# Splitting the softplus of a stick-breaking attention for its triangular sums, with GpSimd's sum, the remainder's product and linear attention's pieces placed anew

## The chip, the cores and the metric

The kernel runs on one core of a Trainium2 chip. The metric is the device time in microseconds of that core; the time before is the median of three executions. Five engines matter: TensorE (PE in the profile, its weight loads are PEld), VectorE (DVE), ScalarE (ACT), GpSimd (POOL) and SyncE (SP), which issues most of the DMAs. Each engine works off its own instructions in order, and engines wait for each other on semaphores.

## The reference, cut to what matters

One layer of a hybrid block over 1024 frames of width 1024: a projection feeds three groups of heads (stick-breaking attention, RWKV-7, gated linear attention), then an output projection and a feed-forward part. The change lies in the stick-breaking attention, with gated linear attention woven into the same loops:

```
z = jnp.einsum('bqhd,bkhd->bhqk', q_blk, kh) * scale
mask = key_pos[None, :] < q_pos[:, None]
log_1m_beta = jnp.where(mask, jax.nn.log_sigmoid(-z), 0.0)
between = lax.cumsum(log_1m_beta, axis=3, reverse=True) - log_1m_beta
weights = jnp.where(mask, jnp.exp(jax.nn.log_sigmoid(z) + between), 0.0)
...
o_intra = jnp.einsum('bhts,bhsv->bhtv', scores, v_c)     # linear attention, 64-frame chunks
S = S * jnp.exp(b_last)[:, :, 0, :, None] + jnp.einsum('bhsk,bhsv->bhkv', k_c * jnp.exp(b_last - b), v_c)
```

With softplus(z) = -log_sigmoid(-z), the weight of a key is exp(z minus the sum of softplus over this key and all later ones). The sum inside a block of 128 keys is a product with a triangular matrix of -1, and the sum over later blocks is a product with a matrix of -1 (`ones`) of a running sum `R`.

## The kernel before, in words

The program has three stages in time: the front (projection and RWKV-7), `heads` (both attentions), and `back` (output projection and feed-forward). `back` is another block of the program and starts when all engines have left `heads`.

`heads` treats the six heads as three pairs (`PAIRS`, index `i`). A pair has 24 units (`UNITS`, index `u`): first 8 units for the first 512 queries, then 16 for the second 512. A unit is one block of 128 keys (`kb`, from the last to the first) for one head of the pair. The blocks on the diagonal are masked and narrower, so a unit is 128, 256, 384 or 512 columns wide (`off` is the first column): per pair 2 each of 128, 256 and 384 wide in either half of the queries, the rest 512 wide, which makes 12 of 512 and 4 of each other width. `span(u)` is the unit's columns.

What each engine does for a unit, in its order:

* TensorE: `scores(u+2)` puts z into one of four PSUM banks `Z`, as two products with operands of type fp32r (`qL`, `qH`) and a mask product; `sums(u)` adds the triangular product of `SP` and, unless the unit is the head's first, the `ones` product of `R`, all in plain f32; then for even `u` `values(u-2)`; then its pieces of linear attention, `gla(i * NU + u)`.
* ScalarE: `exp_of_z(u+2)`, `weight(u)` (the exponential of the finished bank), `log_of_e(u+2)`, then other pieces and its `gla`.
* VectorE: `softplus(u)` (from `E` and the bank `Z` into `SP`), from `u` = 10 of the last pair on one `split_low` of the output projection's operands a unit (`ahead`), at u = 7 and 11 of later pairs `scale` and `mixed_low`, and its `gla`.
* GpSimd: the running sum, `R` new = `R` old + `SP`, a cleared block beside it on the diagonal, a drain, the semaphore `cut`, and its `gla`.

A semaphore counts units: `z`, `log`, `sp` (softplus), `tri_mm` (all sums of a unit in PSUM), `sum` and `cut` (GpSimd), `weight`.

Linear attention is cut into labelled pieces, each with a slot number in the table `SLOTS`; it is done twice (`h` = 0, 1, one for each half of the frames), the second 26 slots later (`LAG`). `gla(n)` issues on an engine all its pieces whose slot is at most `n`. So a slot is a unit, counted through the pairs (24 a pair). Pieces that this text names: on VectorE `scan` 5, `diag0`, `diag1` 7, 8, `qin`, `kout` 8, `keys3` 14, `take0`, `take1` 14, 15, `take3` and `keys5` 18, `take5` 21, `soft_g` 19, `both0`, `both1` 26, 27, `result0`, `result1` 28; on TensorE `turn_k` 9 (waits for `kout`), `level1` 16 (waits for `keys3`, `take1`), `level2` 19 (waits for `keys5`, `take3`), `out` 22 (waits for `take5`); on ScalarE `qin_exp` 6 (waits for `scan`) and `rs` 27 (waits for `both1`); on GpSimd `diff0` to `diff5`, two subtractions each.

## Time and profile before

| | |
|---|---|
| median of three executions | 1580.3 us (1577.7 to 1583.3) |
| the profiled execution's own time | 1584.14 us |
| its span, first to last instruction | 1582.4 us |
| mean granted clock of TensorE | 0.979 of full speed |
| busy: PE, PEld, DVE, ACT, POOL | 93%, 72%, 42%, 33%, 19% of the span |
| `heads` on TensorE, first scores of pair 0 to last values | about 531 to 760 us |

The table's busy shares are averages over stages with different limits; only the stretch of `heads` is touched by the change, 229 us of the span. In a timeline row the first number is the start, the second the duration; TensorE's rows overlap, since one matmul's end runs beside the next one's start, so the cost of a product is the distance from its start to the next start. A plain f32 product is recorded as two matmuls (x2), one with fp32r operands as one.

### The profile page before, as it was taken

How to read it: one execution, taken by the hardware profiler on the slowest of the kernel's cores; microseconds unless marked ns; L12 is line 12 of the kernel's file. 1: busy time of each engine (PE TensorE's matmuls, PEld its weight loads, DVE VectorE, ACT ScalarE, POOL GpSimd, SP SyncE). 2: the span in 40 equal slices, each digit the busy share in tenths (PEclk: the TensorE clock that was granted, in tenths of full speed). 3: DMA queues.
4: the chain of work that ended last, by engine and by line, in shares of the span. 5: the costliest groups of instructions: out<-in, count | busy, mean ns of one | idle time of the engine just before them, and what ended most of it. 6: DMA issues, size and time to landing. Idle time of an engine off the chain costs nothing.

```text
span 1582.4 us, 27309 instructions
## 1 busy us (share of the span) xinstructions
PE 1478.7 (93%) x11281; PEld 1143.1 (72%) x11281; DVE 661.9 (42%) x1058; ACT 523.8 (33%) x936; POOL 305.2 (19%) x412
## 2 busy tenths in 40 slices
PE   5989989989898898989999999999999999999997
PEld 4767767766676554554678788888888888888875
DVE  5244152646563253646275424232332424242336
ACT  4432231424223466777343303122120403021121
POOL 5574624413241251514000100000000000000000
PEclk9999989999999899999999999999999999999999
DMA  5554413423233603004332402112020202111015
GB/s 185 140 146 124 125 42 101 116 57 96 57 87 93 178 2 81 2 1 133 111 132 78 144 16 67 40 40 66 13 93 0 93 13 68 38 61 45 27 40 186
DMA packets 134793, 124.10 MB, mean 78 GB/s; under 512 B 20797, under 2 KB 112122, under 8 KB 134698
## 3 DMA queue, kind: packets, MB, share of 16 engines
q1 hardware_dynamic: 88192, 92.69, 19.0%
q10 hardware_dynamic: 46506, 30.04, 6.8%
q8 instruction: 71, 1.16, 0.3%
q14 instruction: 24, 0.20, 0.0%
HBM read 97.88 MB, written 24.84 MB: 78 GB/s over the span
## 4 chain that ended last, share of the span: by engine, by line
PE 46%; DVE 2%; ACT 1%; DMA 1%; issue 1%; POOLq 0%; SPq 0%; DVEq 0%; ACTq 0%
PE all_ps_b L1990 22%; PE all_ps_b L1967 21%; PE all_ps_b L1572 2%; DMA bk_acc<-in_w_out 1%; POOLq L1592 0%; DVE bk_acc L1855 0%; PE all_ps_b L1960 0%; ACT bk_acc L1758 0%; DVE bk_acc L1865 0%; DVE bk_w1L L1826 0%; DVE all_hL L1871 0%; DVE bk_acc L1851 0%; DVE bk_acc L1922 0%; DVE bk_acc L1925 0%; DVE all_gL L1897 0%
## 5 line engine op out<-in xcount | busy, mean ns | idle before, releaser
L1907 DVE TENSOR_TENSOR bk_acc<-bk_acc,all_ps_b 128x512 f32<-128x512 f32 x128 | 87.9, 687 | 285.3 <-PE all_ps_b L1990 285.3
L1967 PE MATMUL all_ps_b<-all_hH,bk_w1L 128*128 128x512 f32 x512 | 200.1, 391 | 5.1 <-PE all_ps_b L1990 2.2
L1990 PE MATMUL all_ps_b<-bk_w2H,all_gL 128*128 128x512 f32 x512 | 199.8, 390 | 2.5 <-DVE all_gL L1897 2.5
L1990 PE MATMUL all_ps_b<-bk_w2L,all_gH 128*128 128x512 f32 x512 | 199.9, 390 | 0.0
L1990 PE MATMUL all_ps_b<-bk_w2H,all_gH 128*128 128x512 f32 x512 | 199.8, 390 | 0.0
L1967 PE MATMUL all_ps_b<-all_hH,bk_w1H 128*128 128x512 f32 x512 | 199.3, 389 | 0.0
L1967 PE MATMUL all_ps_b<-all_hL,bk_w1H 128*128 128x512 f32 x512 | 199.2, 389 | 0.0
L1200 PE MATMUL fr_ps_F<-fr_hH,fr_wL 128*128 128x512 f32 (+1 forms) x416 | 174.8, 420 | 5.7 <-POOL fr_wL L448 5.5
L448 POOL TENSOR_TENSOR fr_wL<-fr_raw,fr_wH 128x256 fp32r<-128x256 f32 (+1 forms) x208 | 159.6, 798 | 32.6 <-ACT fr_wH L495 29.2
L1200 PE MATMUL fr_ps_F<-fr_hL,fr_wH 128*128 128x512 f32 (+1 forms) x416 | 164.4, 395 | 0.0
L1200 PE MATMUL fr_ps_F<-fr_hH,fr_wH 128*128 128x512 f32 (+1 forms) x416 | 164.3, 395 | 0.0
L1737 ACT CAST bk_w2H<-all_raw 128x1024 fp32r<-128x1024 f32 x32 | 32.8, 1047 | 354.3 <-PEq L1995 351.7
L1967 PEld LDWEIGHTS all_ps_b<-all_hH,bk_w1L 128*128 128x128 f32 x512 | 96.1, 188 | 28.3 <-issue 6.8
L1990 PEld LDWEIGHTS all_ps_b<-bk_w2H,all_gL 128*128 128x128 f32 x512 | 96.5, 189 | 23.0 <-DVE all_gL L1897 2.9
L1990 PEld LDWEIGHTS all_ps_b<-bk_w2H,all_gH 128*128 128x128 f32 x512 | 96.5, 189 | 20.1
L1990 PEld LDWEIGHTS all_ps_b<-bk_w2L,all_gH 128*128 128x128 f32 x512 | 96.4, 188 | 20.1
L1967 PEld LDWEIGHTS all_ps_b<-all_hH,bk_w1H 128*128 128x128 f32 x512 | 96.1, 188 | 20.0
L1967 PEld LDWEIGHTS all_ps_b<-all_hL,bk_w1H 128*128 128x128 f32 x512 | 96.1, 188 | 19.6
L1200 PEld LDWEIGHTS fr_ps_F<-fr_hH,fr_wL 128*128 128x128 f32 (+1 forms) x416 | 77.8, 187 | 31.2 <-POOL fr_wL L448 7.8
L442 POOL CAST fr_wH<-fr_raw 128x1024 fp32r<-128x1024 f32 (+1 forms) x42 | 48.6, 1156 | 255.3 <-PE fr_ps_F L1200 245.7
L1200 PEld LDWEIGHTS fr_ps_F<-fr_hH,fr_wH 128*128 128x128 f32 (+1 forms) x416 | 77.7, 187 | 19.2
L1200 PEld LDWEIGHTS fr_ps_F<-fr_hL,fr_wH 128*128 128x128 f32 (+1 forms) x416 | 78.1, 188 | 15.6
(339 smaller groups left out, 2234.9 us busy)
## 6 DMA issues: line engine op xcount, KB each, us to landing
fr_raw<-in_w_in ACTq DMA_DIRECT2D x37, 512.0 KB, 4.2
bk_raw<-in_w_ff SPq DMA_DIRECT2D x32, 512.0 KB, 4.3
all_raw<-in_w_ff SPq DMA_DIRECT2D x32, 512.0 KB, 4.8
projected<-fr_stage ACTq DMA_DIRECT2D x39, 256.0 KB, 4.4
fr_raw<-in_w_in SPq DMA_DIRECT2D x13, 512.0 KB, 4.2
fr_xt<-in_x SPq DMA_DIRECT2D x8, 512.0 KB, 5.3
bk_acc<-in_x SPq DMA_DIRECT2D x8, 512.0 KB, 3.3
x_after_mixers<-bk_acc SPq DMA_DIRECT2D x8, 512.0 KB, 2.7
```

Source lines behind the costliest of these rows:

```text
L442: pool.tensor_copy(wH[b][:, :, 0:wd], raw[b][:, :, 0:wd]).then_inc(s(f"w_high{b}"), 1)
L448: m = pool.tensor_tensor(wL[b][:, k:k + 2, 0:wd], raw[b][:, k:k + 2, 0:wd], wH[b][:, k:k + 2, 0:wd].bitcast(F32), ALU.subtract)
L1200: m = pe.matmul(F[b][0:wd, :], w[b][:, k, 0:wd], a[:, k, :], start=(k == 0 and q == 0), stop=(k == KB - 1 and q == 2))
L1572: i = pe.matmul(bank[:], m[:, k, ts], w[:, k, :], start=(k == first and q == 0), stop=(k == last and q == 2), skip_group_check=True)
L1737: act.copy(w2H[:, i, :], raw2[i % 2][:]).then_inc(w2_high, 1)
L1907: dve.tensor_tensor(acc[:, j, ds], acc[:, j, ds], ybank[g % 4][:], ALU.add).then_inc(collected, 1)
L1967: m = pe.matmul(bank[s][h][:], w[s][:, k, :], a[:, k, hs], start=(k == 0 and q == 0), stop=(k == KB - 1 and q == 2))
L1990: m = pe.matmul(ybank[g % 4][:], a[:, i, ts], w[:, i, ds], start=(i == 0 and q == 0), stop=(i == FB - 1 and q == 2))
```

## The change

`SP` goes from four buffers to three and stays f32. Two new pairs of buffers hold its two parts: `SPH`, the value rounded to fp32r, written by GpSimd (`tensor_copy`), and `SPL`, the remainder SP - SPH, written by VectorE in a new function `low(u)`. `tri` becomes fp32r. The plain f32 triangular product becomes two fp32r products: `SPH` in `sums(u)`, after the `ones` product, and `SPL` in a new function `remainders(u)`. `sums(u)` is now issued ahead of `scores(u+2)`, and `remainders(u)` behind it. GpSimd's order in a unit is: cast, wait for the remainder (`sp_low`), running sum. VectorE's is: softplus, the other work, linear attention's pieces of two slots earlier (`gla(i * NU + u - 2)`), remainder. ScalarE's program is unchanged; TensorE's and GpSimd's linear-attention pieces keep their slots.

```
-        SP = [r.sb(f"SP{n}", [P, HALF]) for n in range(4)]
+        SP = [r.sb(f"SP{n}", [P, HALF]) for n in range(3)]
+        SPH, SPL = [[r.sb(f"{m}{n}", [P, HALF], F32R) for n in range(2)] for m in ("SPH", "SPL")]
-        tri, ones, eps = r.sb("tri", [P, P]), r.sb("ones", [P, P]), r.sb("eps", [P, 1])
+        tri, ones, eps = r.sb("tri", [P, P], F32R), r.sb("ones", [P, P]), r.sb("eps", [P, 1])
...
                     pool.wait_ge(s("sp"), i * NU + u + 1)
-                    if u >= 4 or i:
+                    if u >= 2 or i:
                         pool.wait_ge(s("tri_mm"), i * NU + u - 1)
+                    pool.tensor_copy(SPH[u % 2][:, span(u)], SP[(i * NU + u) % 3][:, span(u)]).then_inc(s("sp_high"), 1)
+                    pool.wait_ge(s("sp_low"), i * NU + u + 1)
...
-                        dve.wait_ge(s("tri_mm"), i * NU + u - 3)
-                        dve.wait_ge(s("sum"), i * NU + u - 3)
+                        dve.wait_ge(s("sum"), i * NU + u - 2)
...
+                def low(u):
+                    dve.wait_ge(s("sp_high"), i * NU + u + 1)
+                    if u >= 2 or i:
+                        dve.wait_ge(s("tri_mm"), i * NU + u - 1)
+                    dve.tensor_tensor(SPL[u % 2][:, span(u)], SP[(i * NU + u) % 3][:, span(u)],
+                                      SPH[u % 2][:, span(u)].bitcast(F32), ALU.subtract).then_inc(s("sp_low"), 1)
...
-                    gla(i * NU + u)
+                    gla(i * NU + u - 2)
+                    low(u)
...
-                    pe.wait_ge(s("sp"), i * NU + u + 1)
                     z = Z[u % NZ][:, span(u)]
-                    m = pe.matmul(z, tri[:], SP[u % 4][:, span(u)], start=False, stop=True, skip_group_check=True)
                     if not first:
                         pe.wait_ge(s("cut"), i * NU + u - 1)
-                        m = pe.matmul(z, ones[:], rd[:, span(u)], start=False, stop=True, skip_group_check=True)
-                    m.then_inc(s("tri_mm"), 1)
+                        pe.wait_ge(s("log"), i * NU + u + 1)
+                        pe.wait_ge(s("sp"), i * NU + u + 1)
+                        pe.matmul(z, ones[:], rd[:, span(u)], start=False, stop=True, skip_group_check=True)
+                    pe.wait_ge(s("sp_high"), i * NU + u + 1)
+                    pe.matmul(z, tri[:], SPH[u % 2][:, span(u)], start=False, stop=True, skip_group_check=True)
+
+                def remainders(u):
+                    pe.wait_ge(s("sp_low"), i * NU + u + 1)
+                    pe.matmul(Z[u % NZ][:, span(u)], tri[:], SPL[u % 2][:, span(u)], start=False, stop=True, skip_group_check=True
+                              ).then_inc(s("tri_mm"), 1)
...
                 for u in range(-AHEAD, NU + 1):
+                    if 0 <= u < NU:
+                        sums(u)
                     if u + AHEAD < NU:
                         scores(u + AHEAD)
                     if 0 <= u < NU:
-                        sums(u)
+                        remainders(u)
```

TensorE's instructions around units 14 and 15 of pair 0 (512 wide), before: for each unit two scores products of fp32r type, then the f32 triangular product and the f32 `ones` product.

```order
L2801 MATMUL all_ps_b<-early_qL,early_kS 128x512
L2802 MATMUL all_ps_b<-early_qH,early_kS 128x512
L2817 MATMUL all_ps_b<-sb_SP,sb_tri 128x512
L2820 MATMUL all_ps_b<-sb_R,sb_ones 128x512
L2833 MATMUL all_ps_b<-sb_W,sb_vn 64x384 x2
L2801 MATMUL all_ps_b<-early_qL,early_kS 128x512
L2802 MATMUL all_ps_b<-early_qH,early_kS 128x512
```

The same place now:

```order
L2833 MATMUL all_ps_b<-sb_R,sb_ones 128x512
L2835 MATMUL all_ps_b<-sb_SPH,sb_tri 128x512
L2813 MATMUL all_ps_b<-early_qL,early_kS 128x512
L2814 MATMUL all_ps_b<-early_qH,early_kS 128x512
L2839 MATMUL all_ps_b<-sb_SPL,sb_tri 128x512
L2852 MATMUL all_ps_b<-sb_W,sb_vn 64x384 x2
L2833 MATMUL all_ps_b<-sb_R,sb_ones 128x512
```

The scores moved behind the first two sums, and the triangular product stands on both sides of them.

VectorE's instructions of pair 0 from unit 19 on, before: one softplus (`sb_SP`) a unit, with linear attention's pieces of the same unit behind it (`gla_D` are the keys, `gla_A` the takes).

```order
L2739 SCALAR_TENSOR_TENSOR sb_SP<-sb_E,all_ps_b 128x512
L2316 COPY_PREDICATED gla_A<-gla_levels,all_ps_b 128x32x8 x2
L2300 TENSOR_TENSOR gla_D<-gla_D,gla_k 128x8x32
L2301 TENSOR_TENSOR gla_D<-gla_D,gla_q 128x8x32
L2739 SCALAR_TENSOR_TENSOR sb_SP<-sb_E,all_ps_b 128x512
L2389 SCALAR_TENSOR_TENSOR gla_lg<-gla_gate,gla_lg 128x1024
```

The same pieces now, in units 20 and 21:

```order
L2742 SCALAR_TENSOR_TENSOR sb_SP<-sb_E,all_ps_b 128x512
L2317 COPY_PREDICATED gla_A<-gla_levels,all_ps_b 128x32x8 x2
L2301 TENSOR_TENSOR gla_D<-gla_D,gla_k 128x8x32
L2302 TENSOR_TENSOR gla_D<-gla_D,gla_q 128x8x32
L2750 TENSOR_TENSOR sb_SPL<-sb_SP,sb_SPH 128x512
L2742 SCALAR_TENSOR_TENSOR sb_SP<-sb_E,all_ps_b 128x512
L2390 SCALAR_TENSOR_TENSOR gla_lg<-gla_gate,gla_lg 128x1024
L2750 TENSOR_TENSOR sb_SPL<-sb_SP,sb_SPH 128x512
```

A piece of linear attention that stands in a unit is now between that unit's softplus and its remainder, and it is issued two softplus later than before.

## Rows read from the trace of the kernel before

**Rows 1.** Busy time by stretch, one for each pair of heads.

```profile
core 0: us, PE busy (x) PEld busy (x) DVE busy (x) ACT busy (x) POOL busy (x), PEclk, DMA share, GB/s
531.00:605.00 74.00, 72.34 (x939) 42.63 (x939) 34.39 (x60) 48.31 (x98) 28.50 (x44) 0.95 0.30 78
605.00:686.00 81.00, 73.26 (x831) 40.73 (x830) 43.23 (x71) 57.98 (x112) 28.49 (x44) 0.98 0.17 41
686.00:760.00 74.00, 65.66 (x345) 34.73 (x343) 35.45 (x47) 50.53 (x101) 21.52 (x32) 0.93 0.22 72
```

**Rows 2.** Timeline of PE, two 512-wide units of the last pair.

```profile
740.03 0.50 PE L2801 MATMUL all_ps_b<-early_qL,early_kS 128*128 128x512 f32 x1
740.37 0.40 PE L2802 MATMUL all_ps_b<-early_qH,early_kS 128*128 128x512 f32 x1
740.60 1.02 PE L2817 MATMUL all_ps_b<-sb_SP,sb_tri 128*128 128x512 f32 x2
741.46 1.02 PE L2820 MATMUL all_ps_b<-sb_R,sb_ones 128*128 128x512 f32 x2
...
744.59 1.08 PE L2833 MATMUL all_ps_b<-sb_W,sb_vn 128*64 128x512 f32 x4
745.60 0.50 PE L2801 MATMUL all_ps_b<-early_qL,early_kS 128*128 128x512 f32 x1
```

**Rows 3.** Waits in 520 to 770 us: who, for whom, total us, times, longest.

```profile
POOL sb_R L2589 <- DVE sb_SP L2739: 78.7, 38, 6.1
ACT sb_W L2659 <- PE all_ps_b L2820: 43.3, 38, 6.4
DVE sb_SP L2739 <- ACT sb_E L2653: 41.9, 31, 4.8
PE all_ps_b L2817 <- DVE sb_SP L2739: 9.1, 8, 3.9
```

**Rows 4.** Timeline of POOL: a 1024-wide cast, a 128-wide copy, sum and drain.

```profile
224.85 1.04 POOL L442 CAST fr_wH<-fr_raw 128x1024 fp32r<-128x1024 f32 x1 [26.44 <-PE fr_ps_F L1200]
...
531.83 0.29 POOL L2586 COPY sb_R<-sb_SP 128x128 f32<-128x128 f32 x1 [2.97 <-DVE sb_SP L2739]
...
574.86 1.27 POOL L2589 TENSOR_TENSOR sb_R<-sb_R,sb_SP 128x512 f32<-128x512 f32 x1
576.38 0.61 POOL L2427 TENSOR_TENSOR gla_D<-gla_cum 128x256 f32<-128x256 f32 x1 [0.25 <-issue]
```

**Rows 5.** Timeline of DVE and POOL where both read SBUF at once.

```profile
567.70 0.66 DVE L2739 SCALAR_TENSOR_TENSOR sb_SP<-sb_E,all_ps_b 128x512 f32<-128x512 f32 x1
568.44 1.27 POOL L2589 TENSOR_TENSOR sb_R<-sb_R,sb_SP 128x512 f32<-128x512 f32 x1 [2.29 <-DVE sb_SP L2739]
568.61 1.39 DVE L2300 TENSOR_TENSOR gla_D<-gla_D,gla_k 128x256 f32<-128x256 f32 x1 [0.25 <-ACT gla_D L2201]
569.92 0.41 DVE L2301 TENSOR_TENSOR gla_D<-gla_D,gla_q 128x256 f32<-128x256 f32 x1
...
749.84 0.68 DVE L1565 TENSOR_TENSOR all_gL<-all_raw,all_gH 128x512 fp32r<-128x512 f32 x1
750.00 1.66 POOL L2589 TENSOR_TENSOR sb_R<-sb_R,sb_SP 128x512 f32<-128x512 f32 x1 [2.12 <-DVE sb_SP L2739]
```

**Rows 6.** Timeline of DVE: softplus of units 10 and 15, pair 2, and a 1024-wide split.

```profile
719.58 0.42 DVE L2739 SCALAR_TENSOR_TENSOR sb_SP<-sb_E,all_ps_b 128x256 f32<-128x256 f32 x1 [0.57 <-ACT sb_E L2653]
...
732.77 1.23 DVE L1565 TENSOR_TENSOR all_hL<-all_raw,all_hH 128x1024 fp32r<-128x1024 f32 x1 [1.22 <-ACT all_hH L1560]
734.17 0.69 DVE L2739 SCALAR_TENSOR_TENSOR sb_SP<-sb_E,all_ps_b 128x512 f32<-128x512 f32 x1 [0.17 <-ACT sb_E L2653]
```

**Rows 7.** Timeline of DVE and PE at linear attention's last pieces, pair 2.

```profile
710.56 0.75 DVE L2405 SCALAR_TENSOR_TENSOR gla_O<-gla_O,all_col,gla_osq 128x512 f32<-128x512 f32 x1 [4.25 <-ACT gla_osq L2284]
714.08 2.08 PE L2817 MATMUL all_ps_b<-sb_SP,sb_tri 128*128 128x512 f32 x2 [3.88 <-DVE sb_SP L2739]
```

**Rows 8.** Timeline of PE: one level of linear attention (`level2`, pair 0).

```profile
587.62 2.07 PE L2504 MATMUL all_ps_b<-gla_D 32*64 32x32 f32 x128
```

More of the change, by code:

```diff
@@ L2581, in units @@
                     pool.wait_ge(s("sp"), i * NU + u + 1)
-                    if u >= 4 or i:
+                    if u >= 2 or i:
                         pool.wait_ge(s("tri_mm"), i * NU + u - 1)
+                    pool.tensor_copy(SPH[u % 2][:, span(u)], SP[(i * NU + u) % 3][:, span(u)]).then_inc(s("sp_high"), 1)
+                    pool.wait_ge(s("sp_low"), i * NU + u + 1)
                     if kb > 0:
                         if first:
-                            pool.tensor_copy(new[:, off:], SP[u % 4][:, off:]).then_inc(s("sum"), 1)
+                            pool.tensor_copy(new[:, off:], SP[(i * NU + u) % 3][:, off:]).then_inc(s("sum"), 1)
                         else:
                             pool.wait_ge(s("sum"), i * NU + u - 1)
-                            pool.tensor_tensor(new[:, off:], old[:, off:], SP[u % 4][:, off:], ALU.add
+                            pool.tensor_tensor(new[:, off:], old[:, off:], SP[(i * NU + u) % 3][:, off:], ALU.add
                                                ).then_inc(s("sum"), 1)
@@ L2734, in softplus @@
                     dve.wait_ge(s("log"), i * NU + u + 1)
-                    if u >= 4 or i:
-                        dve.wait_ge(s("tri_mm"), i * NU + u - 3)
-                        dve.wait_ge(s("sum"), i * NU + u - 3)
-                    dve.scalar_tensor_tensor(SP[u % 4][:, span(u)], E[u % 4][:, span(u)], CAP, Z[u % NZ][:, span(u)],
+                    if u >= 3 or i:
+                        dve.wait_ge(s("sum"), i * NU + u - 2)
+                    dve.scalar_tensor_tensor(SP[(i * NU + u) % 3][:, span(u)], E[u % 4][:, span(u)], CAP, Z[u % NZ][:, span(u)],
                                              ALU.min, ALU.max).then_inc(s("sp"), 1)
+                def low(u):
[4 more added lines that the diff above has]
+                                      SPH[u % 2][:, span(u)].bitcast(F32), ALU.subtract).then_inc(s("sp_low"), 1)
                 for u in range(NU):
```

## The prediction, made before the changed kernel ran

> **What bounds the kernel now.** The stretches by pair come first [rows 1]: TensorE is busy 72.3 of 74 us in pair 0, 73.3 of 81 in pair 1 and 65.7 of 74 in pair 2, and VectorE and GpSimd stand at about half and a third or less. What is taken from TensorE's path in this stretch is therefore worth time, as long as nobody else becomes later than it. The steady state of the last pair shows the path [rows 2]: two 512-wide units go from 740.03 to 745.60, 5.57 us, with TensorE never idle. So a unit costs 2.79 us. By the distances between starts, one fp32r product of 512 columns takes 0.23 us (740.37 to 740.60) and the f32 triangular product 0.86 (740.60 to 741.46). The waits [rows 3] say who has slack: GpSimd waits 78.7 us for softplus, ScalarE 43.3 us for the sums, VectorE 41.9 us for the logarithm, and TensorE only 9.1 us for softplus. `back` starts when `heads` is left, so a microsecond here is a microsecond of the kernel.
>
> **What the change takes off.** The triangular product goes from 0.86 to two times 0.23, so 0.40 us less per 512 columns. A pair has 12 units of 512, 4 of 384, 4 of 256 and 4 of 128, in columns that is 18 times 512, and 54 in all: 54 x 0.40 = 21.6 us less work on TensorE. A steady unit of it would be 2.39 us.
>
> **What it adds, and where.** Two operations per unit, 72 each. GpSimd's cast is not in the trace at this width; the 1024-wide cast took 1.04 and the 128-wide copy 0.29 [rows 4], so a line between them gives 0.61 for 512 (0.50 for 384, 0.40 for 256). The bounds are 0.52, half of the wide one, and 1.04. VectorE's remainder is the form of the 512-wide split, 0.68 [rows 5], and about 0.55 and 0.42 for the narrower ones, as the 256-wide softplus [rows 6] scales. The work by itself hides beside TensorE. The order doesn't. GpSimd now does, strictly one after another: cast 0.61, hand over 0.08 (softplus ends at 568.36, the sum starts at 568.44 [rows 5]), wait for the remainder 0.68, hand back 0.08, sum 1.27, drain and the next start 0.25 (576.13 to 576.38 [rows 4]). That is 2.97 us per 512-wide unit, against 2.79 before on TensorE and 2.39 there now. This loop runs from GpSimd to VectorE and back and doesn't pass TensorE, so TensorE's gain can't shorten it. The next softplus (0.69) hides under the sum.
>
> Behind the waiting remainder on VectorE stands the next softplus; behind the waiting sum on GpSimd stands the next cast, so both later parts of unit u+1 are held by unit u. The softplus itself waited for the logarithm before, which GpSimd's 78.7 us of waiting covered; that cover is what the loop eats.
>
> Second, other VectorE work stands between softplus and remainder. The rows show what it meets there [rows 5]: a 256-wide multiplication took 1.39 instead of 0.41, because it began 0.17 behind a GpSimd sum and ended 0.29 behind it; and the sum that began 0.16 behind a VectorE split took 1.66 instead of 1.27. One waits until the other is through. The Trainium skill has this as a rule ("SBUF — State Buffer", section "Who interferes with whom"): a VectorE instruction with two SBUF inputs contends with a GpSimd instruction that reads SBUF, and the one that comes second fully blocks. By that rule the trace agrees; without it the unit with a split would cost 2.97, with it 3.4, which is what the rows give too.
>
> Now the sum, by place.
>
> *Pair 2, units 15 to 21 (a 512-wide split each).* After the remainder of unit u-1, VectorE does softplus (0.69), then meets the running sum and splits from 1.35 to 2.03; the cast, ready at 1.60, waits 0.43 for it. 2.97 + 0.43 = 3.40 against 2.79: 7 x 0.61 = **+4.2**.
>
> *Pair 2, units 10 to 14 (splits of 1.23, once `mixed_low`, also 1.2).* The same chain, sum + split + cast + remainder + hand-overs of 0.2, is 2.97 for 256, 3.47 for 384 and 3.99 for 512, so two, two and one of them and 1.2 make 18.1 us; before it took 14.6 (719.58 to 734.17 [rows 6]). Some of it overlaps with waits for loads that stay: I take **+3.0**, between 0 and +3.5.
>
> *Pair 2, units 5 to 8.* VectorE sat 4.25 us before `result0`, waiting for ScalarE's `rs`, with softplus 7 behind it, and TensorE stood 3.88 and then took 2.08 for a product that takes 1.02 elsewhere [rows 7], that is at about half the clock. Two units later, softplus 7 is ahead of that wait. But `rs` now waits on ScalarE for `both1` two units ahead, with `exp_of_z` and the next weight queued behind it, and the four `result` operations (4 x 0.7) hold the remainder of unit 8. The stall is replaced, not removed: **-1.5**, between -4 and +1.
>
> *Pairs 0 and 1.* TensorE sets the pace in most of them, since linear attention's products come on top (2.07 for one level [rows 8], three of them in nine units). The gain of 2 x 18 x 0.40 is **-14.4**. Against it: TensorE's pieces didn't move, while what they wait for did. `level2` (slot 19) needs `take3` and `keys5`, now in unit 20 behind softplus 20: 0.69 + 0.75 + 0.85 behind remainder 19, where TensorE comes after 0.3, so 2.0 each, **+4.0**. `turn_k` (slot 9) needs `kout`, now in unit 10 behind softplus 10, `diag1` and `qin`: 0.42 + 3 x 0.69 = 2.5 less 0.3, **+4.4** for two. `level1` and `out` come out even within 0.2. `rs` in pair 1 waits for `both1` as above, with less to give back: I reckon 12.4 us from remainder 3 to remainder 6 where it is 9.8 now, **+2.6**. About six pieces per pair with two SBUF inputs stand ahead of a remainder and push the cast by 0.6 each, half of it hidden behind levels: 2 x 6 x 0.6 / 2 = **+3.5**. The first units of a pair have nothing to hide cast, remainder and two hand-overs (0.29 + 0.29 + 0.16 for 128): **+2.0** for three pairs. Together +2.1, between -14.4 (all cover holds) and +9.
>
> Sum: 4.2 + 3.0 - 1.5 + 2.1 = +7.8. The profiled execution took 1584.1 us by its own time (1.8 over its span), so it would be 1591.9; that execution is 3.8 above the median of the three, and against the median 1580.3 the forecast is 1588.
>
> **The rivals.**
>
> *TensorE stays the bound, and the change pays.* If VectorE and GpSimd run ahead enough, the gain of pairs 0 and 1 stays but for one kind of stall: -14.4 + 4.2 = -10.2; pair 2 keeps its -1.5 and the loop there comes out even: -11.7, or 1569. For it speak GpSimd's 78.7 us of waiting and that a unit in pairs 0 and 1 has 2.39 + 2.07/3 = 3.08 us of TensorE's work, above the 2.97. It decides from where the loop is under 2.79 us in pair 2, that is if cast and hand-overs come 0.2 cheaper. Against it stands the order of the two engines.
>
> *The moved pieces do their part, and it comes out even.* The stalls of 9.1 us [rows 3] go, the loop costs pair 2 its 4.2, and the rest cancels: within 2 us of now, 1580.
>
> *TensorE's clock falls.* In the front of pair 2 the granted clock was down after an idle stretch of 3.88 us: 2.08 for a product of 1.02 [rows 7]. If pauses of half a microsecond to one in each unit of pair 2 did that, units 10 to 21 would cost 4.78 instead of 3.4, 12 x 1.4 = +17 on top: 1605. The Trainium skill ("TensorE: Matmul & The Clock Gate", section "HAM oscillation — how this bites in real kernels") warns of a clock that is taken back again and again where a kernel pauses regularly. By that rule the loop would cost twice. Against it: the pauses are short, and the stretches of pairs 0 and 2, with idle parts in them, still have 0.95 and 0.93 [rows 1].
>
> *The chain is longer than reckoned everywhere.* If each of the 72 units shows a further 0.1 to 0.2 us of semaphores and blocked reads, it is +8 to +14 more, 1596 to 1602.
>
> **How the numbers follow.** Forecast 0.45 (own range 1580 to 1598), TensorE stays the bound 0.25, even 0.13, clock 0.05, longer chain 0.12. A measurement of this kernel tells 0.3% (4.7 us) from no change. Faster by more than that: the second case and a little of the third, 0.27. Within: most of the third and the low end of the forecast, 0.18. Slower: 0.55. The range for 8 in 10 is 1568 to 1602; it leaves out gains beyond the rival's and the clock case.
>
> **What would show it.** In the profile after: products with `sb_SPH` and `sb_SPL` of 0.23 each start to start, and TensorE's busy time in `heads` down by about 20 us (step 1). GpSimd's sums waiting for `sb_SPL` in nearly every unit, and in pair 2 casts 3.4 us apart (the loop). Casts of 0.61, and of about 1.0 where a split runs (the block). TensorE idle before `turn_k` and `level2` for about 2 us each, waiting for VectorE (the moved pieces). No 3.88 us stall with half clock at unit 7 of pair 2. Pair 2 should be about 80 us long instead of 74. I am wrong if TensorE still has no idle time in pair 2's units 15 to 21, or if casts there are under 2.8 us apart.

## The result, and the profile after

The changed kernel takes **1616.7 us** (median of 4, 1615.4 to 1617.1), the one before in the same sitting 1581.8 (4, 1577.7 to 1585.2): a ratio of **1.0206**, 95% interval 1.0182 to 1.0229. It is about 33 us slower by the ratio, outside the range given. The profiled execution has a span of 1615.4 us against 1582.4 before.

Busy time by stretch in the changed kernel, with the columns of [rows 1]: the three pairs, and last the stretch from its first scores to the first product of the next stage.

```profile
531.00:608.00 77.00, 67.63 (x799) 43.60 (x799) 42.60 (x79) 43.47 (x91) 41.70 (x68) 0.82 0.32 80
608.00:704.00 96.00, 79.25 (x950) 48.87 (x948) 58.75 (x97) 58.97 (x114) 46.18 (x70) 0.88 0.14 34
704.00:793.00 89.00, 74.03 (x365) 39.78 (x365) 56.34 (x79) 54.30 (x105) 37.54 (x57) 0.85 0.17 60
532.40:795.00 262.60, 221.48 (x2114) 131.68 (x2112) 156.97 (x248) 156.65 (x310) 125.11 (x192) 0.85 0.20 56
```

The pairs took 74, 81 and 74 us before and take 77, 96 and 89 now. The last row is the important one. Its counterpart in the kernel before:

```profile
529.90:759.90 230.00, 212.26 (x2114) 119.15 (x2112) 113.07 (x176) 157.49 (x310) 78.52 (x120) 0.95 0.23 64
```

So the whole loss, 262.6 - 230.0 = 32.6 us, lies in this stretch, and it splits in two. TensorE's idle time went from 17.7 to 41.1 (+23.4). Its busy time rose from 212.3 to 221.5, although the change takes 21.6 us of work away, in the same 2114 products: 30.8 us more than the work explains, while the granted clock fell from 0.95 to 0.85. In what follows "excess" means this number, busy time less 212.3 less the change in work.

Most of the excess is the clock, but not all. In the trace before, TensorE is busy for 21.0 us of the stretch at the lower of its two levels (1.2 GHz), in the trace after for 71.4. Half of that is time which the full clock (2.4 GHz) would have saved: 10.5 and 35.7 us, so the clock's part is **25.2 us**. The other 5.6 us go with the number of pauses, 17 of over 0.1 us before and 40 now. A 512-wide product is recorded with 0.40 us where the next one starts after 0.23 [rows 2], and with 0.50 behind a wait, so each pause lays open 0.2 to 0.3 us of a product's end that counts as busy; this is an estimate, and 23 more pauses give about 5 to 6 us by it. A kernel below, e7, bears it out: TensorE has the same work as before, the clock's part is -3.0, and the excess is still +2.5, with 34 pauses.

Waits in the changed kernel, 520 to 800 us, as in [rows 3]:

```profile
POOL sb_R L2593 <- DVE sb_SPL L2750: 42.9, 48, 5.7
DVE sb_SPL L2750 <- POOL sb_SPH L2586: 42.3, 59, 1.9
ACT sb_E L2653 <- PE all_ps_b L2817: 41.2, 26, 3.9
ACT sb_E L2653 <- PE all_ps_b L2814: 34.2, 20, 6.7
PE all_ps_b L2835 <- POOL sb_SPH L2586: 14.3, 13, 2.0
PE all_ps_b L2839 <- DVE sb_SPL L2750: 7.5, 5, 2.9
```

TensorE waits for both halves, and ScalarE waits 75 us for scores, where before it waited 21 us for them and mainly for the sums (43.3). The steady loop of the last pair, timeline of all engines but weight loads:

```profile
770.15 0.78 POOL L2586 CAST sb_SPH<-sb_SP 128x512 fp32r<-128x512 f32 x1 [0.24 <-issue]
...
770.96 0.69 DVE L2750 TENSOR_TENSOR sb_SPL<-sb_SP,sb_SPH 128x512 fp32r<-128x512 f32 x1 [0.50 <-POOL sb_SPH L2586]
...
770.98 0.50 PE L2835 MATMUL all_ps_b<-sb_SPH,sb_tri 128*128 128x512 f32 x1 [0.58 <-POOL sb_SPH L2586]
...
771.73 1.28 POOL L2593 TENSOR_TENSOR sb_R<-sb_R,sb_SP 128x512 f32<-128x512 f32 x1 [0.81 <-DVE sb_SPL L2750]
...
772.16 1.40 DVE L1565 TENSOR_TENSOR all_gL<-all_raw,all_gH 128x512 fp32r<-128x512 f32 x1
...
773.25 0.77 POOL L2586 CAST sb_SPH<-sb_SP 128x512 fp32r<-128x512 f32 x1 [0.24 <-issue]
...
776.35 0.78 POOL L2586 CAST sb_SPH<-sb_SP 128x512 fp32r<-128x512 f32 x1 [0.24 <-issue]
```

Casts stand 3.10 us apart. TensorE pauses here for 0.2 and 0.6 us in every second unit, and from 765 to 790 us its granted clock is 1.00. Now the lower clock, timeline of PE around `level2` of pair 1:

```profile
701.59 1.94 PE L2505 MATMUL all_ps_b<-gla_D 32*64 32x32 f32 x119 [1.48 <-DVE gla_D L2302]
704.66 0.38 PE L2505 MATMUL all_ps_b<-gla_D 32*64 32x32 f32 x9 [1.12 <-issue]
704.96 2.08 PE L2833 MATMUL all_ps_b<-sb_R,sb_ones 128*128 128x512 f32 x2
706.05 1.42 PE L2835 MATMUL all_ps_b<-sb_SPH,sb_tri 128*128 128x512 f32 x1
...
739.86 0.50 PE L2839 MATMUL all_ps_b<-sb_SPL,sb_tri 128*128 128x512 f32 x1 [1.53 <-DVE sb_SPL L2750]
742.33 0.44 PE L2835 MATMUL all_ps_b<-sb_SPH,sb_tri 128*128 128x128 f32 x1 [1.98 <-POOL sb_SPH L2586]
...
744.90 1.97 PE L2852 MATMUL all_ps_b<-sb_W,sb_vn 128*64 128x512 f32 x4
...
752.61 0.58 PE L2839 MATMUL all_ps_b<-sb_SPL,sb_tri 128*128 128x256 f32 x1 [2.87 <-DVE sb_SPL L2750]
```

Two waits of 1.5 and 1.1 us, and the `ones` product lasts 2.08, not 1.02 [rows 2]; two of 1.5 and 2.0 (and one of 1.1), and `values` lasts 1.97, not 1.08. That is the lower level. The kernel before has such stretches too, and not only behind its one long stall of 3.88 us [rows 7]. At the start of pair 1, timeline of PE before, with one row of busy time by stretch behind it (0.50 is the granted clock):

```profile
607.45 0.30 PE L2801 MATMUL all_ps_b<-early_qL,early_kS 128*128 128x128 f32 x1 [1.83 <-issue]
...
612.54 2.66 PE L2530 MATMUL all_ps_b<-gla_osq,all_sb_masks 128*128 128x512 f32 x4 [2.04 <-ACT gla_osq L2277]
```
```profile
613.70:617.12 3.42, 3.42 (x8) 2.19 (x7) 1.02 (x2) 1.18 (x2) 0.87 (x2) 0.50 1.05 223
```

So pauses of 1.8 and 2.0 us came ahead of a lowered clock already there (and at the start of pair 2, 688.8 us). The whole stretch has 4 parts at the lower clock before, its first one included, and 12 now, in all three pairs, and pauses of 1 to 2 us stand in all three pairs too.

### The profile page after: what moved, and what is told of

The parts are those of the page before. It is cut to its first block, busy times and chain, and to the rows that moved or that the text cites. A ratio compares the mean times of both kernels' runs of the same rounds, so it can differ in the third digit from the quotient of the medians.

```text
span 1615.4 us, 27644 instructions
## 1 busy us (share of the span) xinstructions
PE 1487.6 (92%) x11281; PEld 1156.2 (72%) x11281; DVE 707.8 (44%) x1130; ACT 523.3 (32%) x936; POOL 352.6 (22%) x484
## 4 chain that ended last, share of the span: by engine, by line
PE 45%; DVE 2%; ACT 1%; DMA 1%; issue 1%; POOLq 0%; DVEq 0%; ACTq 0%
PE all_ps_b L1990 21%; PE all_ps_b L1967 21%; PE all_ps_b L1572 2%; DMA bk_acc<-in_w_out 1%; POOLq L1592 0%; DVE bk_acc L1855 0%; PE all_ps_b L1960 0%; ACT bk_acc L1758 0%; DVE bk_acc L1865 0%; DVE bk_w1L L1826 0%; DVE bk_acc L1851 0%; DVE all_hL L1871 0%; DVE bk_acc L1922 0%; DVE bk_acc L1925 0%; DVE all_gL L1897 0%
## 5 line engine op out<-in xcount | busy, mean ns | idle before, releaser
L448 POOL TENSOR_TENSOR fr_wL<-fr_raw,fr_wH 128x256 fp32r<-128x256 f32 (+1 forms) x208 | 161.7, 809 | 32.8 <-ACT fr_wH L495 29.4
L1737 ACT CAST bk_w2H<-all_raw 128x1024 fp32r<-128x1024 f32 x32 | 32.9, 1047 | 354.8 <-PEq L1995 351.7
L1990 PEld LDWEIGHTS all_ps_b<-bk_w2L,all_gH 128*128 128x128 f32 x512 | 96.1, 188 | 19.9
L1967 PEld LDWEIGHTS all_ps_b<-all_hL,bk_w1H 128*128 128x128 f32 x512 | 96.1, 188 | 19.7
L442 POOL CAST fr_wH<-fr_raw 128x1024 fp32r<-128x1024 f32 (+1 forms) x42 | 47.3, 1125 | 256.8 <-PE fr_ps_F L1200 247.1
L1895 DVE CAST all_gH<-bk_rect 128x512 fp32r<-128x512 f32 x64 | 27.3, 426 | 146.8 <-ACT bk_rect L1789 146.8
```

Source lines behind the costliest of these rows:

```text
L442: pool.tensor_copy(wH[b][:, :, 0:wd], raw[b][:, :, 0:wd]).then_inc(s(f"w_high{b}"), 1)
L448: m = pool.tensor_tensor(wL[b][:, k:k + 2, 0:wd], raw[b][:, k:k + 2, 0:wd], wH[b][:, k:k + 2, 0:wd].bitcast(F32), ALU.subtract)
L1737: act.copy(w2H[:, i, :], raw2[i % 2][:]).then_inc(w2_high, 1)
L1895: dve.tensor_copy(gH[:, i, hs], g32).then_inc(g_high, 1)
L1967: m = pe.matmul(bank[s][h][:], w[s][:, k, :], a[:, k, hs], start=(k == 0 and q == 0), stop=(k == KB - 1 and q == 2))
L1990: m = pe.matmul(ybank[g % 4][:], a[:, i, ts], w[:, i, ds], start=(i == 0 and q == 0), stop=(i == FB - 1 and q == 2))
```

## The experiments

All figures, in the order of the runs. The medians come from several sittings, so kernels are compared by their ratios. Four executions stand behind most rows (e6 5, e13 10, e15 6); e2's lie between 1556 and 1569 us, e14's between 1602 and 1614. The stretch is the one of above in each profiled execution; all but the first two rows are experiments. "Clock" is the part of the excess that falls to the lower level, worked out as above. The work is that of the changed kernel (-21.6) unless the text says otherwise; 132 fillers are 132 x 0.23 = 30.4 us of it.

| kernel | median us | ratio to before, 95% | stretch | PE idle | excess | of it clock | granted clock |
|---|---|---|---|---|---|---|---|
| before | 1581.8 | | 230.0 | 17.7 | 0 | 0 | 0.95 |
| changed | 1616.7 | 1.0206 [1.0182, 1.0229] | 262.6 | 41.1 | 30.8 | 25.2 | 0.85 |
| e1 changed + fillers | 1610.4 | 1.0156 [1.0139, 1.0173] | 256.8 | 24.0 | 11.7 | 8.3 | 0.92 |
| e2 before, one rounded product | 1562.0 | 0.9866 [0.9834, 0.9897] | 205.8 | 27.1 | 0.4 | -4.7 | 0.97 |
| e3 pieces in own unit | 1635.7 | 1.0314 [1.0288, 1.034] | 282.6 | 54.2 | 37.7 | 26.4 | 0.85 |
| e4 sum free | 1622.6 | 1.0226 [1.0209, 1.0243] | 269.5 | 45.9 | 32.9 | 25.2 | 0.85 |
| e5 scores first | 1605.8 | 1.0141 [1.0114, 1.0167] | 251.4 | 37.2 | 23.6 | 16.3 | 0.88 |
| e6 before, pieces late | 1592.7 | 1.0054 [1.0032, 1.0076] | 242.4 | 25.9 | 4.3 | 5.8 | 0.93 |
| e7 before + extra work | 1604.1 | 1.0127 [1.0103, 1.015] | 247.5 | 32.7 | 2.5 | -3.0 | 0.97 |
| e8 softplus ahead | 1625.6 | 1.0254 [1.0228, 1.0281] | 273.2 | 55.4 | 27.1 | 22.7 | 0.86 |
| e9 split alone | 1627.5 | 1.0268 [1.025, 1.0287] | 278.1 | 55.7 | 31.7 | 22.1 | 0.87 |
| e10 both halves on VectorE | 1652.0 | 1.0425 [1.0399, 1.0452] | 301.1 | 72.8 | 37.6 | 35.8 | 0.80 |
| e11 the same, order of before | 1621.7 | 1.0241 [1.022, 1.0263] | 267.1 | 52.2 | 24.2 | 11.9 | 0.91 |
| e12 before + fillers | 1599.5 | 1.011 [1.0081, 1.0139] | 247.5 | 11.2 | -6.4 | -4.6 | 0.98 |
| e13 e11, sum behind remainder | 1591.8 | 1.0053 [1.0031, 1.0076] | 236.4 | 35.4 | 10.3 | 4.5 | 0.93 |
| e14 e5, read-back last | 1608.0 | 1.015 [1.0092, 1.0207] | 253.1 | 35.7 | 26.7 | 20.3 | 0.87 |
| e15 e7, sum behind remainder | 1597.0 | 1.0094 [1.0062, 1.0125] | 245.3 | 29.5 | 3.5 | -0.7 | 0.96 |
| e16 e5 + fillers | 1607.9 | 1.0141 [1.0114, 1.0168] | 253.3 | 22.2 | 10.0 | 5.6 | 0.93 |
| e17 e13 + fillers | 1598.4 | 1.0078 [1.005, 1.0106] | 243.4 | 19.9 | 2.4 | 0.6 | 0.95 |
| e18 split, sum behind | 1628.7 | 1.0288 [1.0254, 1.0322] | 275.2 | 49.2 | 35.3 | 23.3 | 0.87 |

### Is it the clock? (e1, e12, e16, e17)

The theory: pauses drop TensorE's clock, and that costs more than the pauses. Its rival: the loop over GpSimd sets the time. Useless products in the pauses tell them apart.

```
+ for _ in range(2):     # e1: between ones product and wait for sp_high; others: ahead of scores(u+2)
+     pe.matmul(Z[(u + 2) % NZ][:], kS[0][:, 0:P], qH[0][:, 0:HALF], start=True, stop=True)
```

> The changed kernel with two useless fp32r products of 512 columns per unit (66 of the 72 units, 132 products, 30 us of TensorE's work at 0.23 us each), put into the bank that the next scores will overwrite, between the ones product and the wait for GpSimd's cast. Theory A, pauses lower TensorE's granted clock (0.85 in the attention stretch after, against 0.95 before) and the low clock is most of the loss: the fillers keep the engine at work, the granted clock of the stretch rises to 0.95 or more, and the time falls below 1616, to about 1595 to 1612, although 30 us of work are added. Rival B, the clock follows the pauses but costs nothing, since the chain VectorE - GpSimd - VectorE sets the pace: time 1616 to 1622, whatever the clock does. Rival C, TensorE's work counts in full: 1616 + 30 = 1646.

> The kernel before with the same useless work as in the run with fillers: two 512-column fp32r products in each unit that has scores to give out, here ahead of the scores, some 30 us of TensorE work in all. In the changed kernel these took 6 us off the time. TensorE at the bound before: the fillers cost what they last, less the 17.7 us that the heads stretch idles and what the full clock gives back: 1594 to 1612. If the clock were no matter, and the gain in the changed kernel had another cause that holds here too, the time would be 1575 to 1585.

> The changed kernel with the scores ahead of the sums (1606) and two useless 512-column fp32r products ahead of each unit's scores, some 30 us of TensorE work. The clock in the heads stretch is 0.89 there, TensorE busy 212 us and idle 37. Clock theory: the 20 us of half clock above the work's 191 mostly go and the fillers fit into the idle time but for some 10 us: 1596 to 1608. If the clock were nothing and the gain of fillers in the changed kernel had been an accident of the order, they would cost what they cost the kernel before, about 15 us: 1616 to 1626.

> Both halves on VectorE, the sum waiting (1592), with the same two fillers ahead of each unit's scores. The clock there is 0.93, TensorE busy 202 us, 10 above its work, and idle 37. Clock theory: at most 10 us can be given back and the 30 us of fillers do not all fit into pauses that are waits of a loop: 1590 to 1604. Rival: the idle time takes the fillers whole, so that only the half clock changes: 1582 to 1588, the first version near the kernel before. Rival on the slower side: they delay the scores, on which ScalarE waits: over 1606.

30.4 us of useless work made the changed kernel about 8 us faster by the ratios (5.8 in the stretch), within the 1595 to 1612 of theory A, at its upper end. The fillers' 30.4 us are met from two sources, by the table's pairs of rows. Idle time: 17.1, 15.0, 15.5 and 6.5 us of it (on the changed kernel, e5, e13 and before). Excess given back: 19.1, 13.6, 7.9 and 6.4 us, of which the clock is 16.9, 10.7, 3.9 and 4.6, where the granted clock had been 0.85, 0.88, 0.93 and 0.95. What is left is the change of the stretch: -5.8, +1.9, +7.0, +17.5. The lower the clock was, the more comes back (the last two are alike); this is the clock theory's order. So the lower clock is a real part of the loss and not a way of counting. How much faster the changed kernel would be at the full clock alone is not shown: 17 us of clock came back in e1, and the kernel gained 8 with the fillers in it. e16 and e17 came out within the clock theory's ranges, e12 as well.

### Is it the split's place in the three orders? (e3, e4, e5, e6, e9, e18)

Each undoes placements. Of the changed kernel, e3 undoes the late linear attention on VectorE, e4 the sum's wait, e5 the late scores, e9 all three, e18 all but the sum's wait; e6 is the kernel before with the late pieces alone.

```
- gla(i * NU + u - 2)                            # e3, e9, e18 (and the reverse in e6)
+ gla(i * NU + u)
- pool.wait_ge(s("sp_low"), i * NU + u + 1)      # e4, e9
- sums(u); scores(u + AHEAD); remainders(u)      # e5, e9, e18
+ scores(u + AHEAD); sums(u); remainders(u)
```

> The changed kernel with linear attention's pieces on VectorE back at their own unit (one of the three placements undone). The moved pieces cost TensorE waits of 1.3 to 1.7 us before turn_k and level2, each followed by a stretch at half clock. If they are what costs most (theory E): 1600 or less. If the hand-over chain and the pauses in plain units cost most (theory A): the pieces' own waits for other engines come back in front of the remainder, 1610 to 1625.

> The changed kernel with GpSimd's running sum no longer waiting for the remainder (another placement undone). The loop of a 512-wide unit on GpSimd goes from 0.61 + 0.81 + 1.27 + 0.24 = 2.93 us to 0.61 + 1.27 + 0.24 = 2.12, but the remainder on VectorE, with two SBUF inputs, meets the sum and waits for it (1.27 longer). Theory A with the chain as its cause: the remainder comes 1.3 us later in each unit, TensorE pauses there, the time stays at 1610 to 1630. Theory F, the loop over GpSimd alone is the cause: 1590 to 1600.

> The changed kernel with one placement undone: TensorE gives out the scores of unit u+2 ahead of unit u's sums, so nothing stands between the product with the rounded half and that with the remainder. Clock theory (the 34 us were lost in TensorE's pauses and the half clock behind them): in the changed kernel the scores, about 0.9 us, lie under GpSimd's cast and VectorE's remainder; without them each remainder product waits some 0.8 us longer, but the wait for the rounded half shrinks by as much, so the unit is no shorter, and the pauses get fewer and longer: 1610 to 1640, with the granted clock of the heads stretch at or below the changed kernel's 0.85. Loop theory (the loop over GpSimd's cast, remainder and sum alone sets the unit): no change, 1612 to 1620. Rival: the late scores themselves hurt, since ScalarE's logarithm starts later; then 1590 to 1605.

> The kernel before with the third part of the change alone: linear attention's pieces stand two units later on VectorE. In the changed kernel this placement is worth 18 us (1636 without it). Clock theory: in the kernel before TensorE rarely waits, so the move changes little, 1578 to 1592, the pieces at the ends of the two linear chunks (levels, keys' turn) coming some 3 to 5 us later. Rival: the later pieces make TensorE wait for linear attention's own turns, each wait followed by a stretch at half clock: 1592 to 1605, which would then be a part of the 34 us. Other side: it takes VectorE's pieces out of the softplus's way as it does in the changed kernel: 1565 to 1577.

> The changed kernel with all three placements undone: the sum does not wait for the remainder, the scores stand ahead of the sums, linear attention's pieces stand in their own unit. What is left is the split alone. Measured so far against the changed kernel's 1617: scores ahead 1606, linear attention in its own unit 1636, sum free 1623. If these three add up: 1617 - 11 + 18 + 6 = 1630, range 1620 to 1640; the split alone is then worse than the change, and the placements earned something back. Rival: with the scores ahead the remainder's wait is what VectorE's pieces sit in, so the worth of the late pieces is larger, 1640 to 1655. Rival on the other side: the costs overlap, since the late scores hurt only where VectorE's pieces are late: 1605 to 1620.

> The changed kernel with two placements undone: scores ahead of the sums, linear attention in its own unit; the sum still waits for the remainder. If the waiting sum is worth here what it was in the two pairs measured (7 us with the cast on GpSimd, 30 with both halves on VectorE), then 1627 - 7 to 1627 - 30: 1597 to 1620. Clock and wait theory: TensorE waits for remainders that stand behind linear attention's pieces, as in the split alone (44.7 us), each wait followed by products at half clock; late pieces cure that, so this one is 1612 to 1628, and 10 to 25 above the extra-work kernel's 1597 although TensorE has 21.6 us less to do. Rival: with the contention gone the split is harmless, within 5 us of 1597: then the cost lay in the contention, not in TensorE's waiting.

The late pieces help: 1.0288 to 1.0141 between e18 and e5, 23 us, and 1.0314 to 1.0206 between e3 and the changed kernel, 17 us; e3 is slower than either of its theories said. The late scores hurt: 1.0141 to 1.0206, 10 us, 8.9 of the 11.2 in the stretch as clock. ScalarE's waits for scores are 75 us in the changed kernel and 32 in e5:

```profile
ACT sb_E L2653 <- PE all_ps_b L2817: 19.1, 15, 3.9
ACT sb_E L2653 <- PE all_ps_b L2814: 13.2, 7, 5.1
```

That the scores cover cast and remainder, as the change meant them to, was not borne out; e5's rival held, at the upper end of its range. The placements add up nearly as e9's text had it (1630 expected, 1628 measured). The sum's wait is worth nothing or little with the cast on GpSimd (e9 against e18, e4 against changed: 3 us each, in opposite directions, within the intervals). e18 fell just above the clock and wait theory's 1612 to 1628 (TensorE waits 27.1 us for remainders), far from the rival that called the split harmless. e6 fell on the border between the clock theory and its rival and bears the rival out in kind: TensorE waits 7.6 us for `kout`, one of the late pieces, its idle time is 8.2 us longer and its clock's part is +5.8. So the late pieces cost 8 us where nothing needs them. What they cure is seen in e18. Timeline of e18, pair 2, TensorE, VectorE and GpSimd at linear attention's last pieces:

```profile
743.55 0.49 PE L2835 MATMUL all_ps_b<-sb_SPH,sb_tri 128*128 128x512 f32 x1 [0.28 <-POOL sb_SPH L2586]
...
745.62 0.75 DVE L2406 SCALAR_TENSOR_TENSOR gla_O<-gla_O,all_col,gla_osq 128x512 f32<-128x512 f32 x1 [3.59 <-ACT gla_osq L2285]
...
748.40 0.69 DVE L2750 TENSOR_TENSOR sb_SPL<-sb_SP,sb_SPH 128x512 fp32r<-128x512 f32 x1
...
749.14 0.79 PE L2839 MATMUL all_ps_b<-sb_SPL,sb_tri 128*128 128x512 f32 x1 [5.10 <-DVE sb_SPL L2750]
...
749.75 1.61 POOL L2586 CAST sb_SPH<-sb_SP 128x512 fp32r<-128x512 f32 x1 [6.25 <-DVE sb_SP L2742]
```

The remainder stands behind a piece that waits for ScalarE; TensorE stops for 5.1 us and the next product runs at 0.79 where 0.50 is usual.

### What do the added passes cost by themselves? (e2, e7, e15)

e2 has no remainder at all (one fp32r product of a rounded `SP`, so the output lacks the remainder's part): the least work, 34 us less. e7 and e15 keep TensorE's f32 product of before and add cast and remainder that nobody reads.

```
+ pool.tensor_copy(SPH[u % 2]..., SP[u % 4]...)      # e7, e15: ahead of the sum
+ low(u)                                             # on VectorE, behind gla
+ pool.wait_ge(s("sp_low"), i * NU + u + 1)          # e15 only: sum behind remainder
```

> The kernel before with softplus stored rounded (fp32r) and one fp32r triangular product of it; the remainder is left out of the computation, and there is no new work on GpSimd or VectorE. TensorE has 54 x 0.63 = 34 us less work. Theory A and my sum's first step (less work on TensorE is worth its time as long as nobody is later): 1582 - 34 + up to 8 of waits that come to light = 1548 to 1556. Rival D, TensorE's work in this stretch wasn't the bound at all, the chain through ScalarE and VectorE was: 1570 to 1582.

> The kernel before with GpSimd's cast ahead of its sum and VectorE's remainder behind linear attention's piece added, and nothing that reads them: TensorE multiplies the whole softplus as before. It parts the added work on the two engines from the shorter TensorE work. Clock theory: most of the loss comes of TensorE having to wait in every unit for a rounded half and a remainder; without that it keeps its pace, GpSimd's 0.6 us more in a unit being partly hidden: 1580 to 1596, clock at 0.97 or more. Engine theory (GpSimd's and VectorE's longer queues set the unit whatever TensorE does): 1600 to 1625. Other side, below 1577: not expected by either.

> The kernel before with the cast and the remainder that nobody reads (1604), but GpSimd's sum waits for the remainder. There a 512-column remainder took 1.17 us on average. Contention theory: it falls to 0.7, VectorE's queue is 0.5 us shorter in each long unit, TensorE's waits for the softplus (24 us) shrink: 1588 to 1598, in spite of the sum's wait. Queue theory (the remainder and its wait for the cast stand in VectorE's queue ahead of the next softplus, whatever the pass lasts): 1600 to 1612. Rival, on the slower side: GpSimd's longer loop delays the sum, on which the next unit's all-ones product waits: over 1612.

Less work alone does pay: 34 us less gave 24 in the stretch and 21 by the ratio, which lies between e2's two theories. The passes alone cost 1.0127, 20 us, at a clock of 0.97: this is the engine theory's 1600 to 1625 at its low end, and outside the clock theory's 1580 to 1596. The wait shown in e7 is the softplus, late because it stands behind a remainder that waits for its cast:

```profile
PE all_ps_b L2827 <- DVE sb_SP L2743: 24.1, 24, 4.5
DVE sb_SPL L2748 <- POOL sb_SPH L2587: 19.0, 34, 1.4
```

Before, TensorE's wait was 9.1 [rows 3]. With the sum behind the remainder (e15) it is 15 us. The number is the contention theory's (1588 to 1598), and a 512-wide remainder did go from 1168 to 691 ns; but the gain over e7, 5 us, is not clear of the two intervals, and the other 15 us stay, as the queue theory has it. e15 and e18 differ in TensorE's reading of the two halves, with the order of its products and the smaller number of `SP` buffers that belong to it. This takes 21.6 us of work off and makes the kernel 31 us slower (1.0094 to 1.0288): idle +19.7, excess +31.8, of which clock +24.0.

### Can the loop be taken apart? (e8, e10, e11, e13, e14)

```
+ softplus(u + 1); low(u); gla(i * NU + u)       # e8: VectorE's order; the sum is free
```
```
+ dve.scalar_tensor_tensor(SPH[u % 2]..., E, CAP, Z, ALU.min, ALU.max)   # e10, e11, e13: no cast on GpSimd;
+ dve.scalar_tensor_tensor(SP[(i * NU + u) % 3]..., the same)            # then low(u), then gla
```

In e10 linear attention and scores stand as in the changed kernel, in e11 and e13 as before; in e10 and e11 the sum is free, in e13 it waits for the remainder. e14 is e5 with the five read-back pieces of `ahead` put behind the eight of weights.

> The changed kernel with VectorE's order pipelined: the softplus of unit u+1, then the remainder of unit u, then linear attention's piece of unit u; and GpSimd's sum does not wait for the remainder. No work is added or taken out. Clock theory: TensorE's waits for the rounded half (14.3 us) and the remainder (7.5 us) shrink, and the half clock behind them with them: 1590 to 1606. Loop theory: cast, sum and drain are back to back on GpSimd, 2.6 us a unit where the changed kernel has 3.1: pair 2 gets some 5 us shorter, 1605 to 1612. Rival: the remainder of unit u now stands behind a softplus that waits for the next unit's logarithm, so TensorE waits longer for it: 1625 to 1650.

> The changed kernel without GpSimd in the loop: VectorE writes the rounded softplus, the softplus and the remainder one after the other, then linear attention's piece two units later; GpSimd has only its sum, as in the kernel before. TensorE's order is the changed kernel's. Hand-over theory (the unit is long because softplus, cast, remainder and sum pass through two queues that hold other work, and e7 showed 19 us for that without any loss of clock): two hand-overs go, VectorE has about 0.45 us more in a unit, and TensorE gets its two operands some 1 us earlier: 1570 to 1595. Clock theory (pauses of any kind, the late scores among them, drop the clock): 1590 to 1610. Rival: VectorE, with three passes in a row before its piece, becomes the bound: 1615 to 1640.

> As the run with both halves on VectorE, but with the scores ahead of the sums and linear attention's pieces in their own unit, that is, the kernel before with both halves made on VectorE and its one f32 product replaced by two fp32r ones. Hand-over theory: scores ahead gave 11 us in the changed kernel and late pieces 18 us, the latter because VectorE's pieces stood ahead of the remainder; here they stand behind it in any case, so the old order is the better one: 1562 to 1582, the kernel that may beat both. Clock theory: TensorE has 21.6 us less work than before, and its pauses lower the clock: 1575 to 1595. Rival: the pieces are late, 1595 to 1620.

> As the run with both halves on VectorE and the old order (1622), but GpSimd's sum waits for the remainder. In 1622's trace a 512-column remainder takes 1.4 us because the sum runs beside it, against 0.69 in the changed kernel. Contention theory: 36 such remainders lose 0.7 us each and the 24 shorter ones 0.5, some 35 us of VectorE's time, of which about half lay on the path; VectorE's queue gets free earlier and the time falls to 1590 to 1608. Queue theory (three passes ahead of the piece are the cost, whatever they last): 1612 to 1625. Rival: the sum starts 0.7 us later and the product with the all-ones matrix waits for it: 1625 to 1640.

> The changed kernel with the scores ahead of the sums (1606) and, besides, the order of the pieces loaded and split ahead for the next stage turned round: first the eight of the output weights, last the five that read linear attention's output back. In pair 2 ScalarE waited 5.7 us there for a read-back, with its exponentials queued behind, since the late pieces of linear attention also delay its store. Read-back theory: that wait goes, worth 3 to 5 us and up to 2 more of half clock: 1599 to 1604. Rival: the wait was covered or only moves, since the units with a wide piece (1 to 1.4 us on ScalarE and VectorE) then stand at the end of the pair, ahead of the last weights: 1605 to 1612.

e8's rival came true: the remainder waits behind a softplus that waits for its logarithm, and TensorE waits for the remainder 36 times, 40.6 us. e10 and e11 were far slower than the hand-over theory said, e10 beyond all its rivals. Groups of VectorE's instructions tell why, first of e11, then of e13, which differ in the sum's wait alone (columns: busy us, mean ns, idle before):

```profile
L2750 DVE TENSOR_TENSOR sb_SPL<-sb_SP,sb_SPH 128x512 fp32r<-128x512 f32 x36 | 51.4, 1427 | 3.8
```
```profile
L2751 DVE TENSOR_TENSOR sb_SPL<-sb_SP,sb_SPH 128x512 fp32r<-128x512 f32 x36 | 26.4, 732 | 3.8
```

Where the sum is free to start beside the remainder, the remainder lasts twice as long (e10: 1426). Making the sum wait gave 1.0241 to 1.0053, 30 us, for one wait: the contention theory. That is the rule that the prediction cited from the Trainium skill ("SBUF — State Buffer", section "Who interferes with whom"), and 1427 against 732 ns agree with it. With the contention gone, e13 is 37 us faster than e18, and the best version that computes the whole sum this way. It differs from e18 in two things: no cast on GpSimd (VectorE computes the softplus twice instead, once rounded), and the remainder ahead of linear attention's pieces. Which of the two is worth how much is not shown; a version with GpSimd's cast and the remainder ahead of the pieces was not run. e13 is still 0.3 to 0.8% behind the kernel before; no version that splits beat that one. e10's further 29 us over e11, from late scores and late pieces together, were not taken apart. e14 changed nothing that its wide interval lets one see (it holds e5's ratio): ScalarE's wait for the read-back went from 5.7 to 3.0 us, and 3.3 us for a weight came in its place, so the wait moved.

## Why the prediction was wrong

**The path through the runs**, one step after another, in ratios and as us of the stretch: before to e15 (added passes) +0.94%, +15.3; to e18 (TensorE reads the halves) +1.94%, +29.9; to e5 (late pieces) -1.47%, -23.8; to the changed kernel (late scores) +0.65%, +11.2. Together +32.6. In another order the steps could have other prices.

That the kernel gets slower was forecast (0.55), but by 8 us and not by 33. **The step that failed** is that the sum has no term for TensorE's clock. It stood beside the sum as the rival "TensorE's clock falls", at 0.05, put aside because the pauses were thought short and [rows 1] showed 0.93 to 0.98. The runs show 25.2 us of clock. The waits, taken together, came out as summed: the forecast of +7.8 with 21.6 us of work taken off holds 29.4 us of them, and measured are 23.4 us of idle time and 5.6 of pauses' ends, 29.0. With the clock this is the whole loss: 29.0 - 21.6 + 25.2 = 32.6. This is bookkeeping, with e1 and the other fillers as the proof that the clock's part is real, and the close agreement of the waits is partly luck, as the terms below show.

The rival itself had the wrong place and the wrong pauses. It priced +17 for units 10 to 21 of pair 2. Units 15 to 21 keep the full clock in spite of a pause in every second unit, while pairs 0 and 1 give about 9 us of clock each and pair 2 about 8. The Trainium skill's warning that was weighed there ("TensorE: Matmul & The Clock Gate", section "HAM oscillation — how this bites in real kernels") was right in kind: the clock was taken back again and again. Its example has waits of 3 to 5 us in each round; here pauses of 1 to 2 us, several close together, went with it, and the loop's regular short ones did not.

**What the change takes off**: the work, 21.6, is consistent with e2 (34 us less by the same arithmetic, 33.6 less busy time measured) and not visible in the busy time, where I said it would be, since the clock's part is larger.

**Pairs 0 and 1, "+2.1"**: measured +3 and +15, that is nothing in the sum of both when the clock's 18 are taken off. The term's size was right for the wrong reasons. The late pieces were put down as a cost (`turn_k` +4.4, `level2` +4.0, `result` +2.6) in a sum that took the remainder's wait as covered. The waits at those places are there but smaller (1.32 and 1.48 at `level2`, 1.7 at `turn_k`, once); without the late pieces the kernel is 17 to 23 us slower still (e3, e18).

**The late scores** had no term at all: I priced the move of the remainder's product behind the scores as nothing, and didn't see that the same edit moves the scores behind the wait for the cast, and with them ScalarE's work two units ahead. It costs 10 us.

**The loop over GpSimd**: the mechanism was right and mis-sized, 3.10 instead of 3.40 us a unit, so 7 x 0.31 = 2.2 us and not 4.2. The cast took 0.77 beside a split there, so blocked by 0.16, not 0.43; in the clear it is 0.61 as reckoned (14 of the 36 wide casts; their mean is 0.85, the longest 1.64). The loop was not the main cause, by these 2.2 us. e4 doesn't settle it, since freeing the sum also made the remainder slower (a median of 0.93 instead of 0.62 over all widths).

**Pair 2, "+5.7"**: measured +15, about +7 without the clock. Units 0 to 14 lost most of it: the pauses of 1.5, 2.0 and 2.9 us above. The 3.88 us stall went, as said, and 2.87 at unit 10 took its place. **"Softplus behind the remainder"** was named and priced in the last pair only; e15, which adds cast, remainder and the sum's wait together, is 15 us over all pairs.

## What to carry to other kernels

Before shortening the work of the engine that sets the pace, ask what the new operands wait for: here both halves came through the queues of two other engines in turn, and 22 us less work brought 31 us more time. Count not the pauses alone but the clock after them, and try useless work in the pauses: if the kernel gets faster, the clock is a part of the loss. Look in the kernel before for stretches at the lower clock and for what stands ahead of each: a mean of 0.95 can hide them. When a piece of an engine's order is moved, price what ends up behind its waits as well, and keep two-input VectorE passes away from GpSimd's.

## What the runs showed of the hardware

Pauses of 1 to 2 us, several close together, went with products at 1.2 GHz (2.08 instead of 1.02 us), in the kernel before as well as in the changed one, while pauses of 0.2 and 0.6 us once in 6.2 us did not. The same idle time had different prices: e13 has 35.4 us idle and 4.5 us of clock, e5 37.2 and 16.3; which pauses count was not settled.

A 512-wide subtraction on VectorE with both inputs in SBUF took 1427 ns where GpSimd's sum could start beside it and 732 where the sum waited (e11, e13).

Inside a level of 128 small products, which waited first, TensorE stopped three times for 1.1 to 1.6 us with nothing to wait for ("issue", as at 704.66), which the kernel before doesn't show there. What this is stays open: no run tried it.
